# Relative position bias of a hybrid decoder step: added to the scores by VectorE from a table in row order, in place of two products per head on TensorE

## What is computed

```
def t5_bucket(n):                       # distance -> one of 32 buckets
    n = jnp.maximum(n, 0)
    ...
    large = jnp.minimum(large, N_BUCKETS - 1)
    return jnp.where(n < max_exact, n, large)

logits = jnp.einsum('btngd,btknd->btngk', qg, k_sel).astype(F32) * HEAD_DIM ** -0.5
bias = rel_table.astype(F32)[t5_bucket(q_pos[None, :, None] - idx)]
...
logits = jnp.where(valid[:, :, None, None, :], logits + bias, -jnp.inf)
p = jax.nn.softmax(logits, axis=-1)
out = jnp.einsum('btngk,btknd->btngd', p.astype(v_sel.dtype), v_sel)
```

## Time and profile before

| | us |
|---|---|
| median of 3 runs | 857.04 (856.95 to 860.72) |
| the profiled execution, its own time | 857.15 |
| its span in the profile | 854.8 |

### The profile page before, as it was taken

One profiled execution on the slowest core, in us unless ns is written; L12 is line 12 of the kernel. 1 busy time (PEld: TensorE's weight loads), 2 busy tenths in 40 slices (PEclk: granted clock), 3 DMA queues, 4 the chain that ended last, 5 costly groups with the idle time before them and its releaser, 6 DMA issues.

```text
span 854.8 us, 17930 instructions
## 1 busy us (share of the span) xinstructions
PE 819.4 (96%) x6497; PEld 741.2 (87%) x6497; DVE 570.8 (67%) x1153; ACT 410.6 (48%) x1200; POOL 384.0 (45%) x575
## 2 busy tenths in 40 slices
PE   3999989999999999999999999989999998999998
PEld 3989979699999989999999999956677667898998
DVE  4535777899988988859993536787856358555111
ACT  6646674224554496467455645554445345422100
POOL 2543635209824484549565425139731327501400
PEclk9999999999999999999999999999999999999999
DMA  8312102201101312041205145494653535341422
GB/s 268 80 38 60 62 27 68 76 21 50 51 2 50 98 53 75 26 130 39 82 26 150 37 117 150 130 257 124 158 161 122 162 99 167 107 142 45 142 76 75
DMA packets 69179, 81.31 MB, mean 95 GB/s; under 512 B 20234, under 2 KB 55738, under 8 KB 68842
## 3 DMA queue, kind: packets, MB, share of 16 engines
q1 hardware_dynamic: 64410, 66.58, 25.5%
q0 software_dynamic: 4688, 13.64, 5.8%
HBM read 62.85 MB, written 17.34 MB: 94 GB/s over the span
## 4 chain that ended last, share of the span: by engine, by line
PE 79%; issue 5%; DVE 4%; POOL 4%; ACT 3%; SPq 3%; DMA 2%; POOLq 0%; ACTq 0%; DVEq 0%
PE psum L2095 25%; PE psum L2092 15%; PE psum L1222 12%; PE psum L1991 4%; PE psum L2029 3%; PE psum L1175 3%; PE psum L1191 2%; PE psum L1294 2%; SPq L547 2%; PE psum L1975 2%; PE psum L2011 1%; PE psum L1158 1%; PE psum L1154 1%; PE psum L1160 1%; POOL page_keys L566 1%
## 5 line engine op out<-in xcount | busy, mean ns | idle before, releaser
L2095 PE MATMUL psum<-w_high,xT_high 128*128 128x256 f32 x720 | 204.1, 283 | 1.4 <-ACT psum L1672 1.4
L2095 PE MATMUL psum<-w_low,xT_high 128*128 128x256 f32 x720 | 201.9, 280 | 0.0
L2095 PE MATMUL psum<-w_high,xT_low 128*128 128x256 f32 x720 | 201.6, 280 | 0.0
L1878 DVE TENSOR_SCALAR_CACHE_REDUCE flag<-scores,candidate 128x384 f16<-128x384 f32 (+2 forms) x192 | 181.6, 946 | 6.8
L512 POOL TENSOR_TENSOR w_low<-w_raw,w_high 128x256 fp32r<-128x256 f32 (+1 forms) x168 | 123.0, 768 | 78.5 <-ACT w_high L1560 69.3
L2095 PEld LDWEIGHTS psum<-w_high,xT_high 128*128 128x128 f32 x720 | 127.4, 177 | 3.9 <-ACT psum L1672 1.6
L2095 PEld LDWEIGHTS psum<-w_low,xT_high 128*128 128x128 f32 x720 | 127.6, 177 | 2.3
L2095 PEld LDWEIGHTS psum<-w_high,xT_low 128*128 128x128 f32 x720 | 127.4, 177 | 2.4
L2092 PE MATMUL psum<-xT_high,w_high 128*128 128x384 f32 (+3 forms) x312 | 102.1, 327 | 1.6 <-DVE xT_low L1805 1.2
L2092 PE MATMUL psum<-xT_high,w_low 128*128 128x384 f32 (+3 forms) x312 | 99.7, 319 | 0.0
L2092 PE MATMUL psum<-xT_low,w_high 128*128 128x384 f32 (+3 forms) x312 | 99.6, 319 | 0.0
(11 more groups left out here) (313 smaller groups left out, 1853.5 us busy)
## 6 DMA issues: line engine op xcount, KB each, us to landing
w_raw<-in_w_main SPq DMA_DIRECT2D x40, 512.0 KB, 3.8
x_rows<-in_x_prompt SPq DMA_DIRECT2D x8, 512.0 KB, 5.6
page_keys<-in_cache_kt SPq DMA_DIRECT2D x32, 128.0 KB, 3.5
page_keys<-in_cache_kt POOLq DMA_DIRECT2D x32, 128.0 KB, 5.1
page_values<-in_cache_v SPq DMA_DIRECT2D x32, 128.0 KB, 3.7
page_values<-in_cache_v POOLq DMA_DIRECT2D x32, 128.0 KB, 3.4
x_res<-in_x_prompt SPq DMA_DIRECT2D x32, 128.0 KB
out<-y_rows SPq DMA_DIRECT2D x32, 128.0 KB
```

Source lines behind the costliest of these rows:

```text
L1878: dve.tensor_scalar(JK[:, 0:w], sc, threshold(k), None, op, ALU.add, accum_out=CNT[:, k:k + 1]).then_inc(s["dve_chain"], 1)
L2095: last = pe.matmul(ps(BANK[n], w, rows(i)), x[:, k, row0(i):row0(i) + rows(i)], ww[:, sl, k, 0:w], start=first, stop=final)
```

## The change

The table that goes to DRAM is written with each head's row repeated 128 times (8 x 128 x 383 numbers), and read back so that partition p holds the bias of query row p in right order (`BT`). The antidiagonal matrix, its load and its conversion on GpSimd, the two halves `BH` and `BL` and the two products per head (and piece) are gone. VectorE adds `BT` to the near columns of the scores in PSUM ahead of the maximum, as an instruction of its own, and waits for it (`link`) before the maximum. The wait for the table (`bias_in`) is now VectorE's, at m = 0. The diff, cut to its core:

```diff
-CONSTS_IN = 14 * 16
+CONSTS_IN = 13 * 16
...
-        BRAW, = over(R0_, ("bias_raw", [AH, NEAR], F32))[:1]
-        BL, = over(R0_, ("bias_low", [AH, NEAR], F32R))[:1]
-        VT, BH, PT0, PT1, _e = over(H0, ("values_T", [NT, UW], F32), ("bias_high", [AH, NEAR], F32R),
-                                    ("pT_0", [NT, P], F32), ("pT_1", [NT, P], F32))
+        BT, = over(R0_, ("bias_by_row", [AH, NEAR], F32))[:1]
+        VT, _e = over(H0, ("values_T", [NT, UW], F32))
+        PT0, PT1, _e = over(_e + 8192, ("pT_0", [NT, P], F32), ("pT_1", [NT, P], F32))
...
-        d_ut = nc.dram_tensor("bias_spill", [AH, UL], F32)
+        d_ut = nc.dram_tensor("bias_spill", [AH, P, UL], F32)
...
-                sp.dma_start(BRAW[:, :, :], bass.AP(d_ut, 0, [[1, P], [UL, AH], [1, NEAR]])).then_inc(s["bias_in"], 16)
+                sp.dma_start(BT[:, :, :], bass.AP(d_ut, P - 1, [[UL - 1, P], [P * UL, AH], [1, NEAR]])).then_inc(s["bias_in"], 16)
...
-        def act_bias(act):
-            act.wait_ge(s["bias_in"], 16)
-            act.wait_ge(s["intra_products_ready"], NT * NG)
-            act.activation(BH[:, :, :], BRAW[:, :, :], ACT.Copy).then_inc(s["bias_high_ready"], 1)
...
-                if i == NT - 3:
-                    dve.wait_ge(s["bias_high_ready"], 1)
-                    dve.tensor_tensor(BL[:, :, :], BRAW[:, :, :], f(BH[:, :, :]), ALU.subtract).then_inc(s["bias_low_ready"], 1)
...
                     lg = ps(2 * (m % 2), P * (t + 1))
+                    k0, w = max(t - 1, 0) * P, min(t + 1, 2) * P
+                    if m == 0:
+                        dve.wait_ge(s["bias_in"], 16)
+                    link(dve.tensor_tensor(lg[:, k0:k0 + w], lg[:, k0:k0 + w], BT[:, h, NEAR - w:NEAR], ALU.add))
...
-                    pe.wait_ge(s["bias_low_ready"], 1)
...
-                    k0, k1 = max(c0, (t - 1) * P), min(c0 + n, (t + 1) * P)
-                    if k0 < k1:
-                        for half in (BH, BL):
-                            pe.matmul(ps(bank, k1 - k0, o=k0), ANR[:, :],
-                                      half[:, h, k0 - (t - 1) * P:k1 - (t - 1) * P], start=False, stop=False)
...
-            sp.dma_start(d_ut.ap(), UT[0:AH, :]).then_inc(s["bias_table_out"], 16)
+            sp.dma_start(d_ut.ap(), rep(UT[0:AH, :], P)).then_inc(s["bias_table_out"], 16)
...
-            gp.tensor_scalar(ANR[:, :], ANT[:, :], 1.0, 0.0, ALU.mult, ALU.add)
```

More of the change, by code:

```diff
@@ L131 @@
 NUMBERS_AT = UNITS.index(("hg", 1))
-BIAS_AT = JOB0[LAST] + 12
 QUERIES_AT = JOB0[LAST] + 15
@@ L205, in hymba_step @@
         IDN = sb("ident", [P])
-        ANR = sb("antidiagonal_r", [P], F32R)
         QG = sb("q_gain", [HD])
@@ L329, in hymba_step @@
         assert _e <= cur[0]
-        TRF, ANT, _ = over(cur[0], ("causal_add_f", [P], F32), ("antidiagonal", [P], F32))
+        TRF, = over(cur[0], ("causal_add_f", [P], F32))[:1]
         VN, PN, DG, _e = over(cur[0] - 2048, ("v_new", [UW], F32), ("prob_new", [BR], F32), ("diag", [BR], F32))
@@ L1346, in _ @@
                              (INM[:, :, :], c_masks[:, 0:256]),
-                             (HM[0:BR, :], c_masks[0:BR, 656:674]), (TRF[:, :], c_masks[:, 400:528]), (ANT[:, :], c_masks[:, 528:656])):
+                             (HM[0:BR, :], c_masks[0:BR, 656:674]), (TRF[:, :], c_masks[:, 400:528])):
                 sp.dma_start(dst, src).then_inc(s["const_in"], 16)
@@ L1752, in _ @@
                         chunk(*event)
-                    if n == BIAS_AT:
-                        act_bias(act)
                     if n in BUILD_AT:
```

## The result

| | before | after |
|---|---|---|
| median, us | 857.31 (856.95 to 860.72, 4 runs) | 883.50 (879.01 to 886.22, 4 runs) |
| profiled execution, its span | 857.15, 854.8 | 885.54, 883.7 |
| mean granted clock of TensorE | 1.000 | 0.986 |

The ratio is 1.028 (95% interval 1.025 to 1.031): the change costs 26 us, where 1.3 us of gain was forecast. The forecast range ended at 862.

A forecast was written before the change was run, and what follows sets the result against it. Attention-loop heads were taken as bound variously by TensorE's stream, copies out of PSUM or one head's whole chain. 857.15 + 0 (to 612) - 1.5 (heads 12 to 63) + 0 (write) = 855.6, written as 855.8; range 851 to 862.

The forecast's parts named there:

- the size of the table's write: Near 65 us: the write grows from 12 KB to 1.57 MB, takes 11.7 us and costs 0, up to 6.5.
- a rival with 0.07: Write holds up the search, felt near 318 us: decides from 3.5 us delay; at 10 us, time 862; chance 0.07.
- What a gather loses: GpSimd's gathers beside the write: three or four lose 0.9 us each, 3 us in all.
- 3.5 us free at the chunk products: Search path to TensorE's chunk products at 317.81: waits of 1.4 and 2.1 us would absorb a late search.
- The bound of 10 us: Upper bound on the gathers' total delay beside the write, lower bound 0; at 10 us it costs 6.5.
- VectorE becomes the bound: Loop, heads 0 to 22 and 36 to 47: 25 steps each pay an addition less products; about 863 us; chance 0.09.
- the additions' length: VectorE, ahead of each maximum: 0.416 us for 256 columns, 0.295 for 128; 0.46 and 0.33 with the wait.
- no wait for the table at m = 0: Loop start: the table's read keeps its size, its wait moves from 539.8 to 562, nothing to pay.
- the kinds of step in the loop: Before a head's transposes: TensorE last (gains 0.23 or 0.42), a copy last (nothing), whole chain awaited (costs 0.2 to 0.5).
- heads 57 to 63: Loop's last stretch: +0.8 us, from chains at 57 and 61 and the last scores behind VectorE's splitting.
- copies give way: Heads from 12 on: TensorE's products gained in full, 843.7 us, or half, 850.4; chance of half or more 0.18.
- the page of keys: Head m = 11: TensorE's 1.83 us wait, until about 611.9, absorbs earlier changes; another arrival time would show the prediction wrong.

The follow-up runs named there:

- the two runs with 64 rows an engine: Changed kernel with 64 copies and two reads instead of 128 copies: 870.84 us (1.015); with 128 copies written from 16 partitions instead of 8: 872.92 us (1.016).
- the two loops without bias: Changed kernel with 16 copies but without its 64 additions: 849.95 us (0.990); kernel before without its 144 bias products: 849.63 us (0.989).
- the run with 16 copies: Changed kernel with 16 copies of the table instead of 128, read by 8 DMAs of 16 partitions each: 860.15 us, ratio 1.001.
- the DRAM copies: Changed kernel with the 128 copies made from DRAM, copies or heads in the slowest dimension: 861.51 us both times (1.004 and 1.003).

## Why the prediction was wrong

**The step that failed is the size of the table's write, and the cost of 0 that followed from it** ("at that rate it takes 11.7 us ... with rows of 1.5 KB I take 0.9 each, 3 us in all, and as bounds 0 and 10"). That the write can hold up the gathers was written down as a rival with 0.07, with at most 10 us of delay; the measured delay of the search is 29 us, and the change costs 26. Three parts of the step were off.
- The length: 31 us, not 11.7. The rate of the earlier trace rows belongs to a load into 128 partitions with 4 KB packets. I had no row for a transfer of this form (8 partitions, 1532 B, read again and again), and carried the nearest rate over as if it were a bound. (The term is also 11.4 and not 11.7 us, if both sizes are counted in the profile's KB, 1532 and 512.) The bound should have been worked out for a form that no row shows. Half the engines makes 23 us, as the text said in a sentence by itself; the rest is the price of such a row.
- What a gather loses: I took 0.9 us each, as if it shared engines with the write. It does not share, it stands in line: 16.93 and 11.15 us, and 13.8 in the two runs with 64 rows an engine. The packets show how. Of the 16 pieces of 4096 B of the gather that took 16.93 us, 8 went at once, at 72.8, on the engines that the write left free, and 8 only between 85.6 and 87.3, when 550 to 600 of the 1024 rows were out. Of the next gather 8 went at 91.3 and 8 between 99.3 and 100.8, at the write's end. The Trainium skill, page "DMA: Bandwidth & Descriptors" (Queues, rings and completion order), says that an engine goes round its rings by whole packets, typically of 9 to 17 descriptors and at most 64. The trace is near the upper figure and far from the typical one: the gather got its turn after some 70 rows an engine.
- Who waits, and so the path to TensorE: I had only the search, with 3.5 us free at the chunk products. GpSimd issues gathers and splits weights in one line, so `w_low` came late too. TensorE waited 6.2 us for it, 6.1 for the gathered keys and 2.5 for ScalarE, ran at the lower clock beside these waits, and was 24 us late at 242 and 27 at 342. The 3.5 us did not help.

**The bound of 10 us** was what I could imagine rather than a row. With it the range reached 862; with 128 rows an engine in front of two gathers it had to reach beyond 880. A sum is off as well, without weight: the price of the rival "VectorE becomes the bound" adds up to 864 (857.15 + 5.8 + 1), not 863.

**Right:** that GpSimd's gathers are what the write meets; the additions' length; no wait for the table at m = 0; the kinds of step in the loop and their sums, seven of eight stretches within 0.5 us (heads 36 to 41 with the help of a fall of the clock that was not forecast); that TensorE's 96% were no reason for a gain, and VectorE's additions none for a loss of their own size. **Off by size:** heads 57 to 63, +0.8 forecast and +3.1 measured. The chains there were counted, but not that TensorE, idle 1.18 and 1.01 us in a row, comes back at the lower clock. Whether it does is partly chance, as the two loops without bias show. The rivals "copies give way" and "VectorE becomes the bound" are both refuted by the run with 16 copies (1.001).

Of the prediction's signs of being wrong one came: the page of keys came at another time. The chunk products, which it had at 317.8, came at 344.95.

Open is why 16 copies and the DRAM copies reach the loop 1.9 to 3.8 us late in their profiled executions. The kernel before without its products, whose write is the short one of 12 KB, is 1.5 us late there, and the kernel before itself varies by more between runs.

## What to carry to other kernels

Before a DMA grows, count its rows per engine (the partitions or slowest dimension that it can be dealt over, then rows each) and multiply by the price of a row of that form; if no row of the profile shows the form, the bound is wide. Then ask what is chained through the same engines at that moment: a short gather that a whole engine waits for pays the length of what stands before it (by one trace here, a load of instructions does too). Look at all that the waiting engine does in the same line, not only at the work that the gather feeds. Replicate as little as the reader's access pattern needs (16 copies and 8 reads did the work of 128), and put per-head constants into an operand that is added anyway. Before a microsecond or two in a loop is put down to an edit, see whether the clock fell in one of the two traces.

## What the runs showed of the hardware

- A 1532 B row held a DMA engine 0.21 us when read from SBUF over and over (8 or 16 partitions), 0.072 us from DRAM.
- A gather of GpSimd that came behind a bulk write of 64 rows an engine waited for all of them (13.80 and 13.84 us). Behind 128 rows it got through after some 70 (16.93 us), and the next one after the rest (11.15 us).
- GpSimd stood still for 12.4 us behind a bulk write, from the last thing that it is seen to need (194.7) to its next instruction (207.1); a load of 8192 B of instructions came at 204.9. That this load was what it waited for is inferred from one trace.
- TensorE ran at 1.2 GHz for 3.4 us or twice that after stretches in which it had worked little: 0.81 of the 3.00 us from 800 to 803, with the fall at 803.8, and 0.09 of the 5 from 165 to 170, with the fall at 169.0. The same work does not always bring it: after 1.88 of 3.4 us the clock fell in one version and not in the other. The profiled execution of the kernel before has no fall ahead of its end, but its mean granted clock in other executions was 0.994 to 1.000.
